# A two-phase MLP: up-projected tiles through DRAM, and a down-projection by seven block products for eight

## The chip, the cores and the metric

The kernel runs on one core of one Trainium2 chip. The metric is device microseconds of one execution. Before the change the median of three runs is 2024.57 us (2020.14 to 2024.82).

## What is computed

One layer of a decoder trunk, 1024 tokens of 1024 features, all in float32. Four token mixers run in parallel, are gated and projected back (`w_out`), and then comes an MLP. Only the MLP is changed:

```
h = rms_norm(x, g_mlp[l]) * (1.0 + sc2) + sh2
x = x + gt2 * (jnp.square(jax.nn.relu(h @ w_up[l])) @ w_down[l])
```

`w_up` is 1024 x 4096 (D_FF = 4096), `w_down` is 4096 x 1024. Both matrix products are made to float32 accuracy from three products of split operands: each operand is written as a high part (rounded to `fp32r`) and a low part (what is left), and high x high, high x low and low x high are summed.

## The kernel before

**The unit of TensorE work.** `split_product` (line 658) issues, for each 128-deep slice, three matmuls that stream 512 columns (lines 663, 664 and 665). Each matmul has a 128x128 weight load of its own. In the profile a matmul's name is "output<-one operand, other operand".

**Stages.** `stage_close` (line 676) is the last stage. It projects the mixers' results, multiplies by `w_out`, normalises and turns the token tiles (`turn`, `modulate`), and runs the MLP. Until the MLP begins nothing is changed but one DMA. The MLP has NB = 16 blocks of 256 hidden features, each of two feature tiles f of 128. Tokens are in two halves h of 512, the 1024 output columns in two halves c of 512, and TT = 8 token tiles of 128.

**Up-projection.** Blocks 0 and 1 ("plain") take all 8 block products of (feature tile) x (k half) x (token half). Blocks 2 to 15 take seven products P1, P6, P5, P7, P2, P3, P4 of 12 matmuls each (`up`, line 1222): sums of the quarter blocks of `w_up` (`sum_units`) times sums of the quarter blocks of h (`difference`, nine VectorE steps of 128x2048; `high_difference` on ScalarE and `low_difference` on VectorE split the four results into t_hi and t_lo). VectorE adds the seven results (`combine`), and the ReLU and the square follow.

**Down-projection.** `down` (line 1253) takes, for one block b, one column half c and one token tile, both feature tiles: 6 matmuls into one of four PSUM banks. `accumulate` (line 1513, the add is line 1521) adds the bank to the residual x1 in SBUF. That is 16 x 2 x 8 = 256 adds and 1536 matmuls. `w_down` is multiplied by the gate gt2 (`scale_unit`, line 1372) before it is split.

**What sets the order.** All queues are written out by hand. TensorE does plain(0), plain(1), and then for each b down(b) and up(b+2). A loaded weight block lies in a `tl_unit` buffer; ScalarE copies it to `tl_slot_hi` (`split_slot`, line 1021), and VectorE makes `tl_slot_lo` (`low_slot`, line 1377). There are six slots, used in a ring in the order of `ITEMS`. During down(b) VectorE slips the preparation of up(b+2) between the adds. All waits are on counting semaphores, and each engine does its list in order. SyncE (SP) issues all DMAs of the stage in order, so a DMA that waits holds back those behind it.

## Time and profile before

| | before |
|---|---|
| three runs, median | 2024.57 us (2020.14, 2024.57, 2024.82) |
| profiled execution: span from first to last instruction | 2020.5 us |
| TensorE busy | 1967.2 us (97%), 9416 matmuls recorded |
| VectorE busy | 1264.0 us (63%) |
| ScalarE busy | 706.4 us (35%) |
| DMA | 206.47 MB, mean 102 GB/s |
| TensorE clock, mean granted | 0.995 of full |

The page gives no time of the profiled execution other than its span. The span lies 0.4 us above the lowest of the three runs, 4.1 us below their median and 2.7 us below their mean of 2023.2.

How to read it: a matmul's shown duration (0.39 us) holds its passage through the array, which overlaps that of the next one. What a matmul costs a full queue is the distance between two starts. Counts of the program are taken from the code, since some matmul records can be missing. The MLP's down-projection begins 1400.8 us into the span.

### The profile page before, as it was taken

The page shows a single profiled execution, that of the slowest core. Times are in us where ns is not written, and L with a number is a line of the kernel's source. Part 1 is how long each engine was busy: PE and PEld are TensorE (multiplying, and loading weights), DVE is VectorE, ACT ScalarE, POOL GpSimd, SP SyncE. Part 2 cuts the span into 40 slices and gives each one's busy share as a digit, 9 for nine tenths or more (in the row PEclk, how much of TensorE's full clock was granted, in tenths as well). Part 3 has the DMA queues.
Part 4 walks back from the last instruction along what each step waited for, and adds up shares of the span by engine and source line. Part 5 has one row for each costly group of instructions (what it writes and reads, how often), then busy time and mean ns, then how long its engine had stood idle before and what let it go on. Part 6 is the DMA issues. An engine that isn't in the chain of part 4 may idle for free. (4 is left out here: it accounts for less than half of the span.)

```text
span 2020.5 us, 24310 instructions
## 1 busy us (share of the span) xinstructions
PE 1967.2 (97%) x9416; PEld 1584.5 (78%) x9416; DVE 1264.0 (63%) x1655; ACT 706.4 (35%) x1100; POOL 227.3 (11%) x136
## 2 busy tenths in 40 slices
PE   5999999999999999999999999999999999999999
PEld 4787888878766677877788788787888888888887
DVE  6546666101356476548457587669877777777776
ACT  5411212123466542166654443333232122222221
POOL 0121212112222144121101000000000000000000
PEclk9999999999999999999998999999999999999999
DMA  8354554224311252353122765301111111211112
GB/s 275 96 150 144 160 153 141 89 83 123 123 58 47 68 169 58 105 209 120 47 75 83 257 229 182 115 11 59 57 52 60 47 47 48 68 48 48 48 42 94
DMA packets 197339, 206.47 MB, mean 102 GB/s; under 512 B 9402, under 2 KB 154938, under 8 KB 197226
## 3 DMA queue, kind: packets, MB, share of 16 engines
q1 hardware_dynamic: 197056, 204.85, 32.1%
q8 instruction: 76, 1.25, 0.3%
q14 instruction: 37, 0.30, 0.0%
q10 hardware_dynamic: 170, 0.07, 0.0%
HBM read 157.57 MB, written 47.32 MB: 101 GB/s over the span
## 5 line engine op out<-in xcount | busy, mean ns | idle before, releaser
L663 PE MATMUL dn_ps<-h_hi,dn_hi 128*128 128x512 f32 (+1 forms) x1120 | 453.0, 404 | 15.2 <-PEq L60 4.8
L665 PE MATMUL dn_ps<-h_hi,dn_lo 128*128 128x512 f32 (+1 forms) x1120 | 439.7, 393 | 0.0
L664 PE MATMUL dn_ps<-h_lo,dn_hi 128*128 128x512 f32 (+1 forms) x1120 | 439.5, 392 | 0.0
L663 PEld LDWEIGHTS dn_ps<-h_hi,dn_hi 128*128 128x128 f32 (+1 forms) x1120 | 210.5, 188 | 83.2 <-issue 32.6
L665 PEld LDWEIGHTS dn_ps<-h_hi,dn_lo 128*128 128x128 f32 (+1 forms) x1120 | 210.4, 188 | 47.6
L139 POOL TENSOR_TENSOR dn_lo<-dn_raw,dn_hi 128x1024 fp32r<-128x1024 f32 (+1 forms) x69 | 172.4, 2499 | 661.6 <-ACT dn_hi L135 661.6
L664 PEld LDWEIGHTS dn_ps<-h_lo,dn_hi 128*128 128x128 f32 (+1 forms) x1120 | 210.7, 188 | 43.2 <-issue 1.2
L1521 DVE TENSOR_TENSOR tl_x<-tl_x,mg_ps_y 128x512 f32<-128x512 f32 x256 | 176.0, 688 | 89.4 <-PE mg_ps_y L665 82.7
L156 ACT ACTIVATE dn_out<-dn_ps 128x512 f32<-128x512 f32 (+1 forms) x138 | 81.8, 592 | 422.7 <-PE dn_ps L665 401.6
L663 PE MATMUL mg_ps_y<-tl_slot_hi,tl_u_hi 128*128 128x512 f32 x480 | 187.1, 390 | 1.2 <-issue 1.2
L665 PE MATMUL mg_ps_y<-tl_slot_hi,tl_u_lo 128*128 128x512 f32 x480 | 186.9, 389 | 0.0
L664 PE MATMUL mg_ps_y<-tl_slot_lo,tl_u_hi 128*128 128x512 f32 x480 | 186.8, 389 | 0.0
L1021 ACT ACTIVATE tl_slot_hi<-tl_unit 128x512 fp32r<-128x512 f32 x128 | 77.7, 624 | 134.4 <-DVE tl_unit L1372 108.8
L555 DVE SCALAR_TENSOR_TENSOR ada_sum<-ada,cols,ada_sum 128x256 f32<-128x256 f32 (+1 forms) x140 | 105.6, 754 | 4.7
L663 PEld LDWEIGHTS mg_ps_y<-tl_slot_hi,tl_u_hi 128*128 128x128 f32 x480 | 90.1, 188 | 20.7 <-issue 2.0
L665 PEld LDWEIGHTS mg_ps_y<-tl_slot_hi,tl_u_lo 128*128 128x128 f32 x480 | 90.1, 188 | 18.7
L664 PEld LDWEIGHTS mg_ps_y<-tl_slot_lo,tl_u_hi 128*128 128x128 f32 x480 | 90.1, 188 | 18.6
L1377 DVE TENSOR_TENSOR tl_slot_lo<-tl_unit,tl_slot_hi 128x512 fp32r<-128x512 f32 x128 | 86.5, 689 | 24.8 <-ACT tl_slot_hi L1021 24.8
L1021 ACT ACTIVATE tl_slot_hi<-tl_unit_sum 128x512 fp32r<-128x512 f32 x42 | 26.5, 632 | 172.9 <-DVE tl_unit_sum L1360 146.9
L1071 ACT ACTIVATE tl_u_hi<-tl_square 128x512 fp32r<-128x512 f32 x60 | 33.3, 621 | 142.5 <-PE mg_ps_y L665 127.2
L561 DVE TENSOR_TENSOR mod<-ps_m,cols 128x2 f32<-128x2 f32 x24 | 3.5, 158 | 117.7 <-PE ps_m L474 117.7
L135 ACT ACTIVATE dn_hi<-dn_raw 128x1024 fp32r<-128x1024 f32 (+1 forms) x71 | 73.7, 1040 | 6.1 <-DMA dn_raw<-w_in_dram 6.1
(390 smaller groups left out, 3468.6 us busy)
## 6 DMA issues: line engine op xcount, KB each, us to landing
dn_raw<-w_in_dram SPq DMA_DIRECT2D x70, 512.0 KB, 4.4
ada<-w_ada_dram SPq DMA_DIRECT2D x24, 1024.0 KB, 7.9
proj<-dn_out SPq DMA_DIRECT2D x72, 256.0 KB, 2.3
logits<-dn_out SPq DMA_DIRECT2D x64, 256.0 KB, 2.3
tl_unit<-w_up_dram SPq DMA_DIRECT2D x64, 256.0 KB, 2.9
tl_unit<-w_down_dram SPq DMA_DIRECT2D x64, 256.0 KB, 2.8
mg_gate<-logits SPq DMA_DIRECT2D x19, 512.0 KB, 4.7
wa_qk<-proj SPq DMA_DIRECT2D x6, 1024.0 KB, 8.3
```

The lines of the kernel that those rows point to most:

```text
L135: self.nc.scalar.activation(self.hi_at(j), self.raw_at(j), ACT.Copy).then_inc(self.hi_ready, 1)
L139: self.nc.gpsimd.tensor_tensor(self.lo_at(j), self.raw_at(j), self.hi_at(j).bitcast(F32), ALU.subtract).then_inc(self.lo_ready, 1)
L156: self.nc.scalar.activation(self.out[0:width, h, :], self.ps[0:width, h, :], ACT.Copy).then_inc(self.copied, 1)
L555: ins = nc.vector.scalar_tensor_tensor(out=total, in0=part, scalar=ck, in1=total, op0=ALU.mult, op1=ALU.add)
L561: last = nc.vector.tensor_tensor(k.mod[:, m:m + ADA_COLS], ps_m[:, m:m + ADA_COLS], k.cols[:, V_BADA + m:V_BADA + m + ADA_COLS], ALU.add)
L663: nc.tensor.matmul(out, w_hi[:, t, :], x_hi[:, t, :], start=begin, stop=False, skip_group_check=reopened)
L664: nc.tensor.matmul(out, w_hi[:, t, :], x_lo[:, t, :], start=False, stop=False, skip_group_check=reopened)
L665: mm = nc.tensor.matmul(out, w_lo[:, t, :], x_hi[:, t, :], start=False, stop=end, skip_group_check=reopened)
L1021: nc.scalar.activation(slot_hi[slot(j)][:, :, :], src, ACT.Copy).then_inc(slot_hi_ready, 1)
L1071: nc.scalar.activation(hidden_at(u_hi, b)[:, f, h * HALF:(h + 1) * HALF], square[:, f, h, :], ACT.Copy).then_inc(u_hi_ready, 1)
L1377: nc.vector.tensor_tensor(slot_lo[slot(j)][:, :, :], unit_at(kind, b, key), slot_hi[slot(j)][:, :, :].bitcast(F32), ALU.subtract).then_inc ...
L1521: nc.vector.tensor_tensor(x1[:, tt, cols], x1[:, tt, cols], bank(4 + n % 4), ALU.add).then_inc(summed, 1)
```

## The change

- **Phase one** makes all hidden blocks. The order on TensorE is plain(0), plain(1), then for b = 2, 3, ...: the first four products of b and the last three of b-1, into PSUM banks 0 to 3 for even b and 4 to 7 for odd b. ScalarE does ReLU and square (`finish`), VectorE makes four sums S1 to S4 of a block's four quarters (`sum_hidden`). Three quarters and the four sums, 7 x 256 KB a block, are stored to a DRAM scratch (`store_hidden`).
- **Phase two** is 7 products x 16 blocks = 112 steps of 12 matmuls (4 token tiles x 3). In step n product i = n // 16 adds block t = n % 16. The product stays in four PSUM banks for 16 steps, or for more where products are summed in place. A step needs a hidden tile, loaded from DRAM into one of three `raw_hidden` buffers, and a 128x512 piece of `w_down` or of its sums (`cell`; the sums are made in place by `turn_down`, 64 VectorE operations in steps 14 to 77). Both are split into a ring of nine pairs of buffers (`high_hidden`, `high_cell` on ScalarE; `low_hidden`, `low_cell` on VectorE). `w_down` stays in 64 cells in SBUF and is loaded once.
- **Eviction**: `keep` (ScalarE) and `evict_down` (VectorE) read the banks at the steps of `EVICT_AT`, multiply by the gate (which now is applied here and is saved in DRAM in between) and add to x1. The last four steps are done token tile by token tile. The last eviction is two dependent VectorE operations and then the store.

The diff, cut:

```diff
+        raw_hidden = [at(f"tl_raw_hidden{i}", kb, [P, HALF]) for i, kb in enumerate((64, 66, 68))]
+        kept = at("tl_kept", 0, [P, 4, HALF])
...
+        FIRST_PART, SECOND_PART = (P1, P6, P5, P7), (P2, P3, P4)
         ITEMS = [("plain", b, (f, kh)) for b in range(PLAIN) for f in range(BF) for kh in range(2)]
-        for b in range(NB):
-            ITEMS += [("down", b, (c, f)) for c in range(NH) for f in range(BF)]
-            if b + PLAIN < NB:
-                ITEMS += [("up", b + PLAIN, (p,)) for p in range(7)]
-        FIRST_DOWN = 4 * PLAIN
+        FIRST_UP = len(ITEMS)
+        for b in range(PLAIN, NB + 1):
+            ITEMS += [("up", b, (p,)) for p in FIRST_PART if b < NB]
+            ITEMS += [("up", b - 1, (p,)) for p in SECOND_PART if b > PLAIN]
         PLACE = {item: j for j, item in enumerate(ITEMS)}
+        A11, A12, A22, S1, S2, S3, S4 = range(7)
+        W11, W12, W21, W22 = range(4)
+        DOWN = [(A11, W11), (A12, W21), (S2, W11), (S3, W12), (S1, W11), (S4, W22), (A22, W21)]
+        BY_EVEN = (0, 2, 3, 6)
...
+        NEEDS = sorted([(t, W11, t) for t in range(NB)] + [(NB + t, W21, t) for t in range(NB)]
+                       + [(SUMS_FROM + 2 * t, w, t) for t in range(NB) for w in (W22, W12)])
+        LOAD_OF = {need[1:]: i for i, need in enumerate(NEEDS)}
...
+        EVICT_AT = {36: (1, 0), 39: (1, 1), 42: (1, 2), 45: (1, 3), 52: (2, 0), 54: (2, 1), 56: (2, 2), 58: (2, 3),
+                    68: (3, 0), 71: (3, 1), 74: (3, 2), 77: (3, 3), 84: (4, 0), 86: (4, 1), 88: (4, 2), 90: (4, 3),
+                    100: (5, 0), 102: (5, 1), 104: (5, 2), 106: (5, 3)}
...
+        def wait_ring(eng, m):
+            if m >= 9:
+                eng.wait_ge(step_done, (m - 9) // 2 + 1)
+            elif m in (4, 5):
+                eng.wait_ge(slot_lo_ready, PLACE["up", NB - 1, (P4,)] + 1)
+            else:
+                b, p = {0: (15, P6), 1: (14, P2), 2: (14, P3), 3: (14, P4), 6: (15, P2), 7: (15, P3), 8: (15, P4)}[m]
+                eng.wait_ge(up_done, up_count(b, p))
...
+            def store_hidden(b):
+                sp.wait_ge(quad_ready[0], b + 1)
+                sp.dma_start(k.hidden[A11, b], square[b % 2][:, 0, 0, :]).then_inc(quads_stored[b % 2], 16)
+                sp.wait_ge(quad_ready[1], b + 1)
+                sp.wait_ge(quad_ready[3], b + 1)
+                sp.dma_start(k.hidden[A12:A22 + 1, b].rearrange("s p t -> p s t"), square[b % 2][:, 1]).then_inc(quads_stored[b % 2], 16)
+                sp.wait_ge(hidden_summed, 4 * (b + 1))
+                sp.dma_start(k.hidden[S1:S4 + 1, b].rearrange("s p t -> p s t"), hidden_sum[:, :, :]).then_inc(sums_stored, 16)
+            def load_hidden(n):
+                i, t = n // NB, n % NB
+                a = DOWN[i][0]
+                if n < 3:
+                    sp.wait_ge(slot_lo_ready, PLACE["up", NB - 2, (P3,)] + 1)
+                else:
+                    sp.wait_ge(ring_lo_ready, 2 * (n - 3) + 1)
+                if a <= A22:
+                    sp.wait_ge(quads_stored[t % 2], 32 * (t // 2 + 1))
+                else:
+                    sp.wait_ge(sums_stored, 16 * (t + 1))
+                sp.dma_start(raw_hidden[n % 3][:, :], k.hidden[a, t]).then_inc(hidden_in[n % 3], 16)
...
+            for b in range(PLAIN, NB):
+                if b >= PLAIN + 1 and b + 1 < NB:
+                    load_ups(b + 1)
+                store_hidden(b - PLAIN)
+            for n in range(3):
+                load_hidden(n)
...
+            def finish(b, f, h):
+                q = 2 * f + h
+                own = square[b % 2][:, f, h, :]
...
                 else:
+                    if q == 0:
+                        act.wait_ge(up_done, up_count(b, P2))
+                        act.wait_ge(quads_stored[b % 2], 32 * (b // 2))
+                        act.wait_ge(hidden_summed, 4 * (b - 1))
+                        nc.scalar.activation(own, bank_of(b, 0), ACT.Relu).then_inc(clipped[0], 1)
+                    else:
+                        act.wait_ge(combined[{1: 3, 2: 4, 3: 2}[q]], nth(b))
+                        nc.scalar.activation(own, own, ACT.Relu).then_inc(clipped[q], 1)
+                    act.wait_ge(clipped[q], nth(b))
+                nc.scalar.activation(own, own, ACT.Square).then_inc(quad_ready[q], 1)
...
+            def high_hidden(n):
+                act.wait_ge(hidden_in[n % 3], 16 * (n // 3 + 1))
+                wait_ring(act, 2 * n)
+                nc.scalar.activation(ring_hi[2 * n % 9][:, :], raw_hidden[n % 3][:, :], ACT.Copy).then_inc(ring_hi_ready, 1)
+            def high_cell(n):
+                i, t = n // NB, n % NB
+                w = DOWN[i][1]
+                if i in (0, 1, 5):
+                    wait_cell(act, w, t)
+                else:
+                    act.wait_ge(turned_down, {2: 2 * t + 2, 3: 2 * t + 1, 4: 2 * NB + 2 * t + 2, 6: 2 * NB + 2 * t + 1}[i])
+                wait_ring(act, 2 * n + 1)
+                nc.scalar.activation(ring_hi[(2 * n + 1) % 9][:, :], cell(w, t)[:, :], ACT.Copy).then_inc(ring_hi_ready, 1)
...
+            for p in FIRST_PART[2:4]:
+                split_slot("up", PLAIN, (p,))
             high_difference(3)
+            for b in range(PLAIN, NB + 1):
+                if b > PLAIN:
+                    split_slot("up", b - 1, (P2,))
+                if b > PLAIN + 1:
+                    finish(b - 2, 1, 0)
+                    finish(b - 2, 0, 1)
+                if b > PLAIN:
+                    split_slot("up", b - 1, (P3,))
+                    split_slot("up", b - 1, (P4,))
+                if b < NB:
+                    take_first(b)
+                if b > PLAIN:
+                    finish(b - 1, 1, 1)
                 if b + 1 < NB:
+                    for p in FIRST_PART:
                         split_slot("up", b + 1, (p,))
+                if PLAIN < b < NB:
+                    finish(b - 1, 0, 0)
+            for n in range(3):
+                high_hidden(n)
+                high_cell(n)
+            finish(NB - 1, 0, 0)
+            high_hidden(3)
+            high_cell(3)
+            finish(NB - 1, 1, 0)
+            finish(NB - 1, 0, 1)
+            for n in range(4, STEPS):
+                high_hidden(n)
+                if n - 3 in (NB, 3 * NB, 5 * NB):
+                    keep((n - 3) // NB - 1)
+                high_cell(n)
...
+            def down(n, tt):
+                i, t = n // NB, n % NB
                 cols = slice(tt * P, (tt + 1) * P)
-                for f in range(BF):
-                    j = PLACE["down", b, (c, f)]
-                    pe.wait_ge(slot_lo_ready, j + 1)
-                    last = split_product(nc, bank(4 + n % 4), hidden_at(u_hi, b)[:, f:f + 1, cols], hidden_at(u_lo, b)[:, f:f + 1, cols],
-                                         flat(slot_hi[slot(j)]).unsqueeze(1), flat(slot_lo[slot(j)]).unsqueeze(1), first=(f == 0), last=(f == BF - 1))
-                last.then_inc(down_done, 1)
+                if t == 0:
+                    wait_down_bank(i, tt)
+                pe.wait_ge(ring_lo_ready, 2 * n + 2)
+                a, w = 2 * n % 9, (2 * n + 1) % 9
+                return split_product(nc, down_bank(i, tt), ring_hi[a][:, cols].unsqueeze(1), ring_lo[a][:, cols].unsqueeze(1),
+                                     ring_hi[w][:, :].unsqueeze(1), ring_lo[w][:, :].unsqueeze(1), first=(t == 0 and i not in (2, 3, 5)),
+                                     last=(t == NB - 1), reopened=i in (2, 3, 5))
...
+            for kind, b, key in ITEMS[FIRST_UP:]:
+                up(b, key[0])
+            for n in range(STEPS - LAST_STEPS):
+                for tt in range(4):
+                    last = down(n, tt)
+                    if n % NB == NB - 1 and tt < 3:
+                        last.then_inc(bank_done, 1)
+                last.then_inc(step_done, 1)
+            for tt in range(4):
+                for n in range(STEPS - LAST_STEPS, STEPS):
+                    last = down(n, tt)
+                last.then_inc(bank_done if tt < 3 else step_done, 1)
...
+            def sum_hidden(b):
+                a11, a21, a12, a22 = (square[b % 2][:, f, h, :] for f in range(BF) for h in range(NH))
+                s1, s2, s3, s4 = (hidden_sum[:, n, :] for n in range(4))
                 for q in range(4):
+                    dve.wait_ge(quad_ready[q], b + 1)
                 if b >= 1:
+                    dve.wait_ge(sums_stored, 16 * b)
                 else:
+                    dve.wait_ge(up_done, 4 * PLAIN)
+                nc.vector.tensor_tensor(s1, a21, a22, ALU.add).then_inc(hidden_summed, 1)
+                nc.vector.tensor_tensor(s3, a11, a21, ALU.add).then_inc(hidden_summed, 1)
+                dve.wait_ge(hidden_summed, 4 * b + 1)
+                nc.vector.tensor_tensor(s2, a11, s1, ALU.add).then_inc(hidden_summed, 1)
+                dve.wait_ge(hidden_summed, 4 * b + 3)
+                nc.vector.tensor_tensor(s4, a12, s2, ALU.add).then_inc(hidden_summed, 1)
...
             difference(8)
+            low_difference(1)
+            for n in (1, 2, 3):
+                sum_units(PLAIN, n)
+            for p in (P1, P6):
+                low_slot("up", PLAIN, (p,))
+            low_difference(2)
+            sum_units(PLAIN, 4)
+            for p in (P5, P7):
+                low_slot("up", PLAIN, (p,))
             difference(9)
+            low_difference(3)
+            for b in range(PLAIN, NB + 1):
+                if b > PLAIN:
+                    low_slot("up", b - 1, (P2,))
+                if b > PLAIN + 1:
+                    combine(b - 2, 5)
+                    combine(b - 2, 4)
+                if b > PLAIN:
+                    low_slot("up", b - 1, (P3,))
+                    low_slot("up", b - 1, (P4,))
+                if b < NB:
+                    combine(b, 1)
+                sum_hidden(b - 2)
+                if b + 1 < NB:
+                    for n in (1, 2, 3):
+                        sum_units(b + 1, n)
+                    for p in (P1, P6):
+                        low_slot("up", b + 1, (p,))
+                    sum_units(b + 1, 4)
+                    for p in (P5, P7):
+                        low_slot("up", b + 1, (p,))
+                if b < NB:
+                    combine(b, 2)
+                    combine(b, 3)
+            for n in range(3):
+                low_hidden(n)
+                low_cell(n)
+            combine(NB - 1, 5)
+            combine(NB - 1, 4)
+            low_hidden(3)
+            low_cell(3)
+            sum_hidden(NB - 1)
+            for n in range(4, STEPS):
+                where = EVICT_AT.get(n)
+                if where:
+                    evict_down(*where, 0)
+                if 0 <= n - SUMS_FROM < 4 * NB:
+                    turn_down(n - SUMS_FROM)
+                if where:
+                    evict_down(*where, 1)
+                low_hidden(n)
+                if where:
+                    evict_down(*where, 2)
+                low_cell(n)
+                if where:
+                    evict_down(*where, 3)
+            for tt in range(4):
+                evict_down(6, tt, 0)
+                evict_down(6, tt, 1)
```

Two places of the order show it. On **TensorE**, after the last matmuls of plain(1), before the change (names: `tl_u` is the hidden block, `tl_slot` a weight block):

```order
L665 MATMUL mg_ps_y<-tl_h_hi,tl_slot_lo_9659 128x512
L663 MATMUL mg_ps_y<-tl_slot_hi_9650,tl_u_hi 128x512
L664 MATMUL mg_ps_y<-tl_slot_lo_9656,tl_u_hi 128x512
L665 MATMUL mg_ps_y<-tl_slot_hi_9650,tl_u_lo 128x512
```

and with the change:

```order
L665 MATMUL mg_ps_y<-tl_h_hi,tl_slot_lo_9659 128x512
L663 MATMUL dn_ps<-tl_h_hi,tl_slot_hi_9650 128x512
L664 MATMUL dn_ps<-tl_h_lo,tl_slot_hi_9650 128x512
L665 MATMUL dn_ps<-tl_h_hi,tl_slot_lo_9656 128x512
```

The 96 matmuls of down(0) that stood between plain(1) and the first product of block 2 are gone from this place.

On **VectorE**, before the change, from the last `difference` on (L1445 is `low_difference`, L1357 to L1363 `sum_units`):

```order
L1441 TENSOR_TENSOR tl_t_full_9683<-tl_t_full_9683,tl_h_lo 128x2048
L1445 TENSOR_TENSOR tl_t_lo_9677<-tl_t_full_9681,tl_t_hi_9673 128x2048
L1445 TENSOR_TENSOR tl_t_lo_9678<-tl_t_full_9682,tl_t_hi_9674 128x2048
L1521 TENSOR_TENSOR tl_x_9643<-tl_x_9643,mg_ps_y 128x512
L1445 TENSOR_TENSOR tl_t_lo_9679<-tl_t_full_9683,tl_t_hi_9675 128x2048
L1521 TENSOR_TENSOR tl_x_9643<-tl_x_9643,mg_ps_y 128x512 x2
```

and with the change, from `low_slot` of P5 and P7 of block 2 to `low_slot` of P1 of block 3 (L1558 is `low_slot`, L1622 and L1626 the last `difference` and `low_difference`, L1635 `combine`, L1662 to L1667 `sum_hidden`, L1542 to L1548 `sum_units`):

```order
L1558 TENSOR_TENSOR tl_slot_lo_9658<-tl_unit_sum_9672,tl_slot_hi_9652 128x512
L1558 TENSOR_TENSOR tl_slot_lo_9659<-tl_unit_9664,tl_slot_hi_9653 128x512
L1622 TENSOR_TENSOR tl_t_full_9685<-tl_t_full_9685,tl_h_lo 128x2048
L1626 TENSOR_TENSOR tl_t_lo_9681<-tl_t_full_9685,tl_t_hi_9677 128x2048
L1635 TENSOR_TENSOR tl_first_product_9689<-tl_first_product_9689,dn_ps 128x512
L1662 TENSOR_TENSOR tl_hidden_sum<-tl_square_9686 128x512
L1663 TENSOR_TENSOR tl_hidden_sum<-tl_square_9686 128x512
L1665 TENSOR_TENSOR tl_hidden_sum<-tl_square_9686,tl_hidden_sum 128x512
L1667 TENSOR_TENSOR tl_hidden_sum<-tl_square_9686,tl_hidden_sum 128x512
L1542 TENSOR_TENSOR tl_unit_sum_9672<-tl_unit_9670,tl_unit_9671 128x512
L1545 TENSOR_TENSOR tl_unit_sum_9673<-tl_unit_sum_9672,tl_unit_9668 128x512
L1548 TENSOR_TENSOR tl_unit_9670<-tl_unit_9668,tl_unit_9670 128x512
L1558 TENSOR_TENSOR tl_slot_lo_9660<-tl_unit_9668,tl_slot_hi_9654 128x512
```

Two long and eight short operations now stand between the slots of block 2 and the first slot of block 3.

On **ScalarE**, with the change, the last three `split_slot` of phase one (L1152), with `finish` (L1196 the ReLU, L1198 the square) of block 14 between them; for blocks 2 to 15 the three products that they serve are P2, P3 and P4:

```order
L1152 ACTIVATE tl_slot_hi_9655<-tl_unit_9669 128x512
L1196 ACTIVATE tl_square_9686<-tl_square_9686 128x512
L1198 ACTIVATE tl_square_9686<-tl_square_9686 128x512
L1196 ACTIVATE tl_square_9686<-tl_square_9686 128x512
L1198 ACTIVATE tl_square_9686<-tl_square_9686 128x512
L1152 ACTIVATE tl_slot_hi_9650<-tl_unit_9668 128x512
L1152 ACTIVATE tl_slot_hi_9651<-tl_unit_9671 128x512
```

Before the change VectorE did the squares, and a down-projection stood between the up-projections of two blocks; now the last three products of block 14 and of block 15 follow one another with nothing between.

## Rows read from the trace of the kernel before

**Rows 1.** The page, engines in total and the groups of instructions (line, engine, names, count | busy, mean ns | idle before).

```profile
PE 1967.2 (97%) x9416; PEld 1584.5 (78%) x9416; DVE 1264.0 (63%) x1655; ACT 706.4 (35%) x1100; POOL 227.3 (11%) x136
...
L1521 DVE TENSOR_TENSOR tl_x<-tl_x,mg_ps_y 128x512 f32<-128x512 f32 x256 | 176.0, 688 | 89.4 <-PE mg_ps_y L665 82.7
```

**Rows 2.** Stretch 1500 to 1600 us, busy time by engine, clock, DMA share, GB/s.

```profile
1500.00:1600.00 100.00, 100.00 (x443) 82.81 (x442) 76.45 (x119) 25.06 (x44) 0.00 (x0) 1.00 0.18 56
```

**Rows 3.** All waits of TensorE from 1300 us to the end.

```profile
PE mg_ps_y L1208 <- DVE tl_xn L1397: 2.1, 2, 1.5
PE mg_ps_y L663 <- issue: 1.2, 1, 1.2
```

**Rows 4.** Timeline of TensorE, first and last of 28 matmuls in a row (start, us).

```profile
1499.72 0.39 PE L663 MATMUL mg_ps_y<-tl_slot_hi,tl_u_hi 128*128 128x512 f32 x1
...
1505.84 0.39 PE L663 MATMUL dn_ps<-tl_h_hi,tl_slot_hi 128*128 128x512 f32 x1
```

**Rows 5.** The tile tl_u_hi: TensorE's matmuls on it, first and last start.

```profile
L663 PE MATMUL mg_ps_y<-tl_slot_hi,tl_u_hi x480: 388/389/468, 1400.8 to 1994.8; 128*128 128x512 f32 x160
```

**Rows 6.** Timeline of VectorE around the start of down(0) and in up(2).

```profile
1398.84 2.29 DVE L1441 TENSOR_TENSOR tl_t_full<-tl_t_full,tl_h_lo 128x2048 f32<-128x2048 f32 x1
1401.05 4.49 DVE L1445 TENSOR_TENSOR tl_t_lo<-tl_t_full,tl_t_hi 128x2048 fp32r<-128x2048 f32 x2
...
1426.44 2.50 DVE L1484 TENSOR_TENSOR tl_u_lo<-tl_square,tl_u_hi 128x512 fp32r<-128x512 f32 x4
...
1435.37 0.68 DVE L1458 TENSOR_TENSOR tl_square<-tl_first_product,mg_ps_y 128x512 f32<-128x512 f32 x1
1436.08 0.69 DVE L1461 TENSOR_TENSOR tl_square<-tl_square,mg_ps_y 128x512 f32<-128x512 f32 x1
```

**Rows 7.** Timeline of ScalarE in the same stretch.

```profile
1398.30 0.60 ACT L1057 ACTIVATE tl_square<-mg_ps_y 128x512 f32<-128x512 f32 x1 [2.50 <-PE mg_ps_y L665]
1401.16 1.92 ACT L1075 ACTIVATE tl_t_hi<-tl_t_full 128x2048 fp32r<-128x2048 f32 x1 [2.27 <-DVE tl_t_full L1441]
...
1425.77 2.20 ACT L1071 ACTIVATE tl_u_hi<-tl_square 128x512 fp32r<-128x512 f32 x4 [8.91 <-DVE tl_square L1478]
```

**Rows 8.** TensorE after idle times elsewhere: timeline, and stretches with the clock.

```profile
39.34 0.80 PE L663 MATMUL dn_ps<-h_hi,dn_hi 128*128 128x512 f32 x1 [4.33 <-DVE h_lo L578]
39.94 0.63 PE L664 MATMUL dn_ps<-h_lo,dn_hi 128*128 128x512 f32 x1
...
44.63 0.47 PE L663 MATMUL fr_open_ps<-h_hi,dn_hi_x 128*128 128x512 f32 x1
...
902.53 0.47 PE L663 MATMUL dn_ps<-h_hi,dn_hi 128*128 128x512 f32 x1 [2.50 <-PEq L60]
902.84 0.39 PE L664 MATMUL dn_ps<-h_lo,dn_hi 128*128 128x512 f32 x1
...
1085.67 0.72 PE L1907 MATMUL wa_ps_second<-ident,wa_prob 128*128 128x128 f32 x3 [2.06 <-ACT wa_probT L1852]
...
1086.00:1088.00 2.00, 2.00 (x12) 2.00 (x10) 2.00 (x1) 0.51 (x1) 1.46 (x1) 0.50 0.70 205
...
1094.00:1096.00 2.00, 2.00 (x6) 1.61 (x6) 1.83 (x12) 0.00 (x0) 0.00 (x0) 0.50 0.00 0
```

**Rows 9.** DMA issues (count, KB, us to landing), and a stretch with many in flight.

```profile
tl_unit<-w_down_dram SPq DMA_DIRECT2D x64, 256.0 KB, 2.8
...
mix<-cv_acc SPq DMA_DIRECT2D x1, 1024.0 KB, 7.8
...
mix<-sb_yT SPq DMA_DIRECT2D x1, 1024.0 KB, 4.3
...
0.00:25.00 25.00, 9.95 (x41) 8.02 (x41) 11.37 (x23) 15.10 (x32) 1.26 (x10) 1.00 0.99 325
```

**Rows 10.** The end: last matmul and last add, from the timelines of both engines.

```profile
2016.97 0.39 PE L665 MATMUL mg_ps_y<-tl_slot_hi,tl_u_lo_last 128*128 128x512 f32 x1
...
2017.40 0.69 DVE L1521 TENSOR_TENSOR tl_x<-tl_x,mg_ps_y 128x512 f32<-128x512 f32 x1 [0.67 <-PE mg_ps_y L665]
```

541 lines of the change are left out of this document (287 added, 254 removed).

## The prediction, made before the changed kernel ran

> **What bounds the kernel now.** I read the engine totals first, then a stretch of the MLP, then TensorE's waits, then the distance of its matmuls. TensorE is busy 97% of the span, VectorE 63%, and VectorE's idle time before the adds of the down-projection is spent waiting for TensorE [rows 1]. Between 1500 and 1600 us TensorE is busy 100.00 of 100.00 us at full clock while VectorE has 24 us free, ScalarE 75, and the DMA engines are used to 18% [rows 2]. From 1300 us to the end TensorE waits 3.3 us in all [rows 3]. So the MLP takes the number of matmuls times their distance. That distance is 6.12 us over 27 matmuls, 0.2268 us, the same in down- and up-projections, which follow each other in that stretch [rows 4]. The MLP's part from down(0) on begins at 1400.8 [rows 5] and the last matmul starts at 2016.97 [rows 10]: 616.2 us for 2711 steps of 0.2268 = 614.9, and 1.3 us more, which is the wait for "issue" [rows 3]. Matmuls are the only currency here, as long as everything else stays hidden.
>
> **What is removed.** The down-projection has 16 x 2 x 8 x 6 = 1536 matmuls before, and 112 x 12 = 1344 after. The up-projection keeps its count. 192 matmuls x 0.2268 = **43.5 us** less. VectorE's 256 adds [rows 1], its 64 gate multiplications and the splitting of hidden blocks in phase one go too. They were hidden and are worth nothing by themselves.
>
> **Prices of the added work.** A VectorE operation on 128x512 occupies the engine 0.60 us when the next is independent (four take 2.50, the last 0.69), and 0.71 when the next reads its result; one on 128x2048 2.29 [rows 6]. A ScalarE operation on 128x512 takes 0.52 to the next and about 0.62 to its result (four take 2.20), one on 128x2048 1.92 [rows 7]. A signal from TensorE reaches another engine about 0.2 us after the next matmul could have started. This follows from the last matmul at 2016.97 and its add at 2017.40, 0.43 later [rows 10]. A product or step is 12 matmuls, T = 2.72 us.
>
> **Phase one in its steady part.** Per block of 7 products (19.05 us) VectorE has 7 low slots, 4 sums of weights, 5 combinations and 4 hidden sums, 20 operations or 12 to 14 us. ScalarE has 16, or 8.5 to 10. The orders leave each weight slot ready three products or more before its use. DMA moves 4 loads and 7 stored quarters of 256 KB, 2.9 MB per 19.05 us, 151 GB/s, where 325 has been moved [rows 9]. Cost: nothing. Cover: the lead of three products.
>
> **The start of phase one: a stall.** Before, the 96 matmuls of down(0), 21.8 us, hid the end of the `difference` chain. Now block 2 begins at 1400.8 and P1 of block 3, four products later, wants to start at 1411.7. VectorE, in order: P5's slot of block 2 can be written only when TensorE leaves the slot, at 1400.8. ScalarE sees that at 1401.0, does ReLU and square of block 1 (0.65 and 0.52), then the split, done at 1402.8. Two low slots (1.2) put `difference(9)` at 1404.1. It takes 2.29, ScalarE's high part 1.92 and hand-overs 0.08, so `low_difference(3)` starts at 1408.4. Then come 2.2 for it, one combination (0.6), four hidden sums (0.6, 0.6, 0.7, 0.6), three sums of weights (0.7, 0.6, 0.6), and the low slot of P1 (0.69). This slot is ready at 1416.3. **Stall 4.7 us** (bounds: 0 if some operations overlap better, 7 if the DMAs of the new weights are late too). Later slots of block 3 follow at 0.6 to 1.2 and need 2.72.
>
> **The clock after it.** After 4.33 us of idleness in the front stage the following 11 matmul distances were 0.43 us, from 39.94 to 44.63, and then 0.23 again; after 2.50 us of idleness following dense work the distance was 0.23 at once; after 2.06 us following small matmuls the granted clock was 0.50 until 1096 [rows 8]. So 12 matmuls at 0.43 cost 12 x 0.20 = **2.4 us**, the value that I take since the idle time is nearest. The ends are 0 (the row at 902.53) and 5 (half of the ten us at 0.50). The Trainium skill ("TensorE: Matmul & The Clock Gate", Part 1) holds that the half-rate clock is the default and sustained activity lifts it. By that rule a cold start after this stall is to be expected, and it gives no reason for the fast restart at 902.53.
>
> **The end of phase one: a second stall.** The last products of block 14 and block 15 are neighbours. The slot of P3(15) comes, on ScalarE, behind `finish` of two quarters of block 14, whose sums can be made only when P4(14) is done. From there: 0.2 signal, 0.7 combination, 0.63 ReLU, 0.54 square, 0.63 ReLU, 0.54 square, 0.63 split, 0.73 low slot: 4.7 us, where TensorE needs it after one product, 2.72. **Stall 2.0 us**, too short for the clock if the 2.50 row holds. In all other blocks four products of the next block lie between, so the same chain is hidden.
>
> **The first steps of phase two.** Steps 0 to 3 are prepared under P3 and P4 of block 15. Step 4 is behind `sum_hidden(15)`, which waits for ScalarE's last squares and for the 1 MB store of S1 to S4 of block 14. Such a store took 4.3 or 7.8 us [rows 9]. My count has step 4 ready 0 to 1 us late. I take **0.5**, bounds 0 and 4.
>
> **Steady phase two.** VectorE has two low parts a step and in steps 14 to 77 one sum, 3 x 0.60 = 1.8 of 2.72 us; with the densest eviction (4 operations in 3 steps, steps 68 to 79) 2.6 plus dependent pairs, about even with TensorE, and nearly three steps of ring stand against it. ScalarE has 1.1. A hidden tile's cycle with three buffers is landing + split + low part, 2.8 [rows 9] + 1.5 = 4.3 us in three steps, 8.2. Changes of product wait for `keep`, which runs bank by bank under the other banks. Cost: nothing.
>
> **The tail.** The last eviction is two dependent operations instead of one: **0.7 us**.
>
> **The small parts**: saving the gate adds one 512 KB store during the branch merging, where DMA has room; nothing.
>
> **Sum.** -43.5 + 4.7 + 2.4 + 2.0 + 0.5 + 0.7 = -33.2 us. Against the profiled span, 2020.5 - 33.2 = 1987.3. The median of the runs shown is 4.1 above that span, their mean 2.7; I add 2.7 and predict **1990.0 us**.
>
> **Rivals.**
> - *No stalls*: the orders overlap better than I count and the whole 43.5 us stay. 2020.5 - 43.5 = 1977, or 1980 for the runs. Against it: the list of VectorE operations between the slots is fixed. Chance 0.12.
> - *A bound in the middle of phase two*: in steps 14 to 31 a step loads a hidden tile and two cells, 786 KB in 2.72 us, 289 GB/s. 325 were moved for 25 us by transfers of up to 1 MB [rows 9]. If 256 KB transfers reach only 240, those 16 steps take 3.3 us each, 9 us more, and the evictions at steps 68 to 79 may add 3. Result 2002, up to 2008 with longer stalls at the change of phase. Chance 0.17.
> - *Slower*: the transfers of one step run one after another, not side by side. Three at 2.8 us [rows 9] are 8.4 us a step; the 16 steps then cost 16 x 5.7 = 91 us more, 2081. It decides from 33/16 = 2.1 us more a step, that is when DMA gives less than 164 GB/s there. Against it: 325 GB/s in the first 25 us, on the same queue. The Trainium skill ("DMA: Bandwidth & Descriptors", Bandwidth) advises transfers of 1 MiB and more for three quarters of the peak, which speaks against this change's 256 KB pieces; its fit of about 2.0 us plus bytes / 436 GB/s gives an estimate of 2.6 us for one of them alone, and if nothing overlapped the sum would be near this rival's. Chance 0.06.
> - *The matmuls saved are no time*: the new waits take back all of it (within 0.3%, 6 us, about what a measurement of this kernel can tell). It would need some 30 us of stalls beyond those counted, 0.27 us at every step of phase two. Chance 0.05.
>
> The forecast itself has 0.60. **Range**: 1978 to 2008. It holds the forecast with its bounds (1982 to 2000), most of the no-stall case and the middle rival; left out are the last two rivals and the edges. Faster 0.89, the same 0.05, slower 0.06.
>
> **What the profile after would show.** 192 matmuls fewer, distance 0.227 in both phases; down-projection about 304.8 us in 112 steps. TensorE's waits: one on `tl_slot_lo` of about 4.7 us near 1412, with half clock for 2 to 5 us behind it, one of 2 us some 250 us later on `tl_slot_lo`, and little on `tl_ring_lo`. The last add would end about 1.8 us after the start of the last matmul (0.43 + 0.71 + 0.69). It would be wrong if TensorE waits on `tl_ring_lo` in every step (DMA landings above 6.7 us in steps 14 to 31, or VectorE at its limit from 14 to 77), if the distance of the matmuls rises though nothing waits, or if the wait near 1412 is absent.

## The result and the profile after

The changed kernel took **1988.78 us** (median of four runs, 1987.47 to 1990.35) beside 2022.36 us for the kernel before (2020.00 to 2024.82): ratio 0.9829, 95% interval 0.9815 to 0.9843. Its profiled execution has a span of 1988.6 us. The prediction was 1990.0 us, and 1987.3 for the span.

The page of the changed kernel, engines in total (busy us, share, instructions), two groups of the MLP (busy, mean ns | idle before), and the DMA issues of the MLP (count, KB each, us to landing):

```profile
PE 1927.7 (97%) x9224; PEld 1551.3 (78%) x9224; DVE 1191.7 (60%) x1555; ACT 831.3 (42%) x1314; POOL 227.2 (11%) x136
...
L1227 ACT ACTIVATE tl_ring_hi<-tl_cell 128x512 fp32r<-128x512 f32 x112 | 70.6, 630 | 140.7 <-PE mg_ps_y L665 126.5
...
L1217 ACT ACTIVATE tl_ring_hi<-tl_raw_hidden 128x512 fp32r<-128x512 f32 x112 | 69.3, 619 | 21.2 <-DMA tl_raw_hidden<-hidden 21.1
...
tl_raw_hidden<-hidden SPq DMA_DIRECT2D x112, 256.0 KB, 2.7
...
tl_unit<-w_up_dram SPq DMA_DIRECT2D x64, 256.0 KB, 3.2
hidden<-tl_hidden_sum SPq DMA_DIRECT2D x16, 1024.0 KB, 4.9
tl_cell<-w_down_dram SPq DMA_DIRECT2D x64, 256.0 KB, 5.1
```

TensorE has 192 matmuls fewer than in [rows 1] and is still busy 97% of the span. VectorE lost 72 us of work, ScalarE gained 125; neither shows in the time. Read the two groups by what released them. ScalarE's splits for phase two were idle 126.5 us waiting for TensorE to leave a slot of the ring, and only 21.1 us for a hidden block to land. So TensorE sets the pace of phase two and the transfers don't.

All waits of TensorE from 1300 us to the end (us in all, count, longest), the counterpart of [rows 3]:

```profile
PE mg_ps_y L663 <- DVE tl_slot_lo L1558: 6.3, 2, 4.5
PE mg_ps_y L1377 <- DVE tl_xn L1578: 2.1, 2, 1.5
PE dn_ps L663 <- DVE tl_ring_lo L1699: 0.5, 1, 0.5
```

The waits on `tl_xn` were there before. The 1.2 us for "issue" are not there any more. New are two waits on `tl_slot_lo`, 4.5 and 1.8 us, and 0.5 us on the ring. The timeline of TensorE shows where (start, length, wait in brackets):

```profile
1364.25 1.09 PE L1377 MATMUL mg_ps_y<-ident,tl_xn 128*128 128x128 f32 x8 [0.58 <-DVE tl_xn L1578]
...
1418.80 0.80 PE L663 MATMUL mg_ps_y<-tl_h_hi,tl_slot_hi 128*128 128x512 f32 x1 [4.46 <-DVE tl_slot_lo L1558]
1419.39 0.63 PE L664 MATMUL mg_ps_y<-tl_h_lo,tl_slot_hi 128*128 128x512 f32 x1
...
1423.97 0.39 PE L663 MATMUL mg_ps_y<-tl_t_hi,tl_slot_hi 128*128 128x512 f32 x1
...
1673.51 0.50 PE L663 MATMUL mg_ps_y<-tl_h_hi,tl_slot_hi 128*128 128x512 f32 x1 [1.82 <-DVE tl_slot_lo L1558]
...
1690.66 0.50 PE L663 MATMUL dn_ps<-tl_ring_hi,tl_ring_hi 128*128 128x512 f32 x1 [0.54 <-DVE tl_ring_lo L1699]
...
1984.33 0.39 PE L665 MATMUL mg_ps_y<-tl_ring_hi,tl_ring_lo 128*128 128x512 f32 x1
```

The first stall is in front of P1 of block 3, the second in front of P3 of block 15. The 12 matmuls of P1(3) take 5.17 us, from 1418.80 to 1423.97, instead of 12 x 0.2268 = 2.72: that is the price of the clock, 2.45 us. The windows of the same kernel show it (us; busy and count of PE, PEld, DVE, ACT, POOL; granted clock, DMA share, GB/s), and below them phase two where it loads most:

```profile
1416.00:1418.00 2.00, 0.00 (x0) 0.00 (x0) 1.97 (x4) 0.35 (x1) 0.00 (x0) 0.75 0.44 163
1418.00:1420.00 2.00, 1.20 (x3) 1.01 (x4) 2.00 (x5) 2.00 (x5) 0.00 (x0) 0.50 1.00 290
1420.00:1422.00 2.00, 2.00 (x7) 1.52 (x6) 1.97 (x4) 0.36 (x1) 0.00 (x0) 0.50 0.65 203
1422.00:1424.00 2.00, 2.00 (x7) 1.58 (x6) 1.67 (x3) 0.00 (x0) 0.00 (x0) 0.55 0.00 0
1424.00:1426.00 2.00, 2.00 (x10) 1.65 (x9) 0.69 (x1) 1.80 (x4) 0.00 (x0) 1.00 0.84 252
...
1700.00:1750.00 50.00, 50.00 (x223) 41.40 (x222) 35.30 (x56) 25.65 (x45) 0.00 (x0) 1.00 0.92 309
1750.00:1800.00 50.00, 50.00 (x222) 41.44 (x221) 42.09 (x68) 20.91 (x37) 0.00 (x0) 1.00 0.57 180
```

The stretch 1700 to 1750 moves 309 GB/s and TensorE is busy all of its 50.00 us at full clock. TensorE does steps 8 to 25 in it, and the loads run ahead: SyncE issues 37 cells and 20 hidden blocks there, as dense as the 36 and 18 that steps 14 to 31 need in 49 us. Phase two as a whole runs from the start of step 0's first matmul at 1679.1 to that of the last at 1984.33, 305.2 us for 1344 matmuls: 304.6 for 1343 distances, and the 0.5 us wait.

VectorE's timeline shows the chain behind the first stall:

```profile
1406.52 2.28 DVE L1622 TENSOR_TENSOR tl_t_full<-tl_t_full,tl_h_lo 128x2048 f32<-128x2048 f32 x1
...
1410.79 2.29 DVE L1626 TENSOR_TENSOR tl_t_lo<-tl_t_full,tl_t_hi 128x2048 fp32r<-128x2048 f32 x1 [1.98 <-ACT tl_t_hi L1212]
1413.00 0.68 DVE L1635 TENSOR_TENSOR tl_first_product<-tl_first_product,dn_ps 128x512 f32<-128x512 f32 x1
...
1418.06 0.68 DVE L1558 TENSOR_TENSOR tl_slot_lo<-tl_unit,tl_slot_hi 128x512 fp32r<-128x512 f32 x1
...
1985.48 0.69 DVE L1755 TENSOR_TENSOR tl_x<-tl_x,tl_gated_product 128x512 f32<-128x512 f32 x1
```

VectorE is not short of time. It is busy with a list in a poor order: `low_difference(3)`, a combination and four hidden sums stand ahead of the slot that TensorE wants at 1414.3. The slot is finished at 1418.74, and P1(3) starts at 1418.80. The last row ends at 1986.17, 1.84 us after the last matmul's start; before it was 1.12 [rows 10].

**A sum from trace to trace.** The front stages, which nobody changed, differ by some us between executions, so I measure from the first TensorE instruction of the last token tile's turn to the end. Before that is 2020.5 - 1361.77 = 658.7 us, after it 1988.6 - 1364.25 = 624.35: **34.4 us less**. The parts: -43.5 matmuls, +4.5 and +2.45 for the first stall and its clock, +1.8, +0.5, +0.7 for the tail, -1.2 for the "issue" wait gone, together -34.75. The front of this execution is 2.5 us later, which is why the whole span shows only 31.9.

### The profile page after: what moved, and what is told of

It is laid out like the page before. It is cut to its first block and busy times, and to the rows that moved or that the text cites. A ratio compares the mean times of both kernels' runs of the same rounds, so it can differ in the third digit from the quotient of the medians.

```text
span 1988.6 us, 24178 instructions
## 1 busy us (share of the span) xinstructions
PE 1927.7 (97%) x9224; PEld 1551.3 (78%) x9224; DVE 1191.7 (60%) x1555; ACT 831.3 (42%) x1314; POOL 227.2 (11%) x136
## 5 line engine op out<-in xcount | busy, mean ns | idle before, releaser
L1227 ACT ACTIVATE tl_ring_hi<-tl_cell 128x512 fp32r<-128x512 f32 x112 | 70.6, 630 | 140.7 <-PE mg_ps_y L665 126.5
L664 PE MATMUL mg_ps_y<-tl_ring_lo,tl_ring_hi 128*128 128x512 f32 x320 | 124.6, 389 | 0.0
L663 PE MATMUL mg_ps_y<-tl_ring_hi,tl_ring_hi 128*128 128x512 f32 x320 | 124.6, 389 | 0.0
L665 PE MATMUL mg_ps_y<-tl_ring_hi,tl_ring_lo 128*128 128x512 f32 x320 | 124.6, 389 | 0.0
L1699 DVE TENSOR_TENSOR tl_ring_lo<-tl_cell,tl_ring_hi 128x512 fp32r<-128x512 f32 x112 | 77.3, 690 | 64.6 <-ACT tl_ring_hi L1227 63.8
L1558 DVE TENSOR_TENSOR tl_slot_lo<-tl_unit,tl_slot_hi 128x512 fp32r<-128x512 f32 x78 | 52.2, 689 | 60.5 <-ACT tl_slot_hi L1152 60.5
L1694 DVE TENSOR_TENSOR tl_ring_lo<-tl_raw_hidden,tl_ring_hi 128x512 fp32r<-128x512 f32 x112 | 76.8, 686 | 12.6 <-ACT tl_ring_hi L1217 12.3
L1217 ACT ACTIVATE tl_ring_hi<-tl_raw_hidden 128x512 fp32r<-128x512 f32 x112 | 69.3, 619 | 21.2 <-DMA tl_raw_hidden<-hidden 21.1
L665 PE MATMUL mg_ps_y<-tl_t_hi,tl_slot_lo 128*128 128x512 f32 x196 | 76.3, 389 | 0.0
L664 PE MATMUL mg_ps_y<-tl_t_lo,tl_slot_hi 128*128 128x512 f32 x196 | 76.3, 389 | 0.0
L663 PE MATMUL mg_ps_y<-tl_t_hi,tl_slot_hi 128*128 128x512 f32 x196 | 76.3, 389 | 0.0
```

The lines of the kernel that those rows point to most:

```text
L663: nc.tensor.matmul(out, w_hi[:, t, :], x_hi[:, t, :], start=begin, stop=False, skip_group_check=reopened)
L664: nc.tensor.matmul(out, w_hi[:, t, :], x_lo[:, t, :], start=False, stop=False, skip_group_check=reopened)
L665: mm = nc.tensor.matmul(out, w_lo[:, t, :], x_hi[:, t, :], start=False, stop=end, skip_group_check=reopened)
L1217: nc.scalar.activation(ring_hi[2 * n % 9][:, :], raw_hidden[n % 3][:, :], ACT.Copy).then_inc(ring_hi_ready, 1)
L1227: nc.scalar.activation(ring_hi[(2 * n + 1) % 9][:, :], cell(w, t)[:, :], ACT.Copy).then_inc(ring_hi_ready, 1)
L1558: nc.vector.tensor_tensor(slot_lo[slot(j)][:, :, :], unit_at(kind, b, key), slot_hi[slot(j)][:, :, :].bitcast(F32), ALU.subtract).then_inc ...
```

## The experiments

The theory: TensorE's matmuls are the only currency, and the stalls at the two changes of phase come from the order of work on VectorE and ScalarE. Rivals: the saving has another source, VectorE as a whole is too slow there, or the transfers of phase two are near their limit. "The sum" below is the stretch just defined, from one profiled execution of each kernel; the changed kernel has 624.35. In a second execution of the same kernel (experiment 5) it is 624.9, so differences of about 0.5 us say nothing.

**1. VectorE's order at the start of phase one.** `low_difference(3)`, `combine(2, 1)` and `sum_hidden(0)` go behind the four low slots of block 3.

```diff
             difference(9)
-            low_difference(3)
...
-                if b < NB:
+                if PLAIN < b < NB:
                     combine(b, 1)
-                sum_hidden(b - 2)
+                if b > PLAIN:
+                    sum_hidden(b - 2)
...
+                if b == PLAIN:
+                    low_difference(3)
+                    combine(b, 1)
+                    sum_hidden(b - 2)
```

(`sum_units` waits in block 3 for one low slot in addition, since the order no longer implies it.)

> At the start of phase one VectorE prepares block 3 (sums of weights and four low slots) before low_difference(3), combine and sum_hidden(0). Theory (time is matmuls x 0.2268 us plus three stalls): the wait of 4.5 us before P1(3) and the 12 slow matmuls behind it (2.6 us) both go, about 7 us less than the changed kernel, some 1981.6 us; no wait on tl_slot_lo but the one of 1.8 us near the end of phase one. Rival (the start is bound by the DMA of the new weights or by the ReLU of block 1, VectorE only shows it): the wait stays, with another releaser, and the time stays within 1 us of 1988.8. A third case: P4(2) now waits for t_lo of the fourth difference, 1 to 3 us back.

Measured 1980.15 us (1977.02 to 1984.69), ratio 0.9791 (0.9774 to 0.9808), an interval that lies apart from the changed kernel's. TensorE's waits in the MLP's part:

```profile
PE mg_ps_y L663 <- DVE tl_slot_lo L1560: 1.8, 1, 1.8
...
PE dn_ps L663 <- DVE tl_ring_lo L1701: 0.5, 1, 0.5
```

The 4.5 us wait is gone, and with it the slow clock: the sum is 617.4, 7.0 us less, for 4.5 + 2.45. No operation was saved, only the order changed, so the stall was one of order and not of VectorE's speed.

**2. ScalarE's order at the end of phase one.** The splits for P3(15) and P4(15) go ahead of `finish` of block 14.

```diff
-                if b > PLAIN + 1:
+                if PLAIN + 1 < b < NB:
                     finish(b - 2, 1, 0)
                     finish(b - 2, 0, 1)
                 if b > PLAIN:
                     split_slot("up", b - 1, (P3,))
                     split_slot("up", b - 1, (P4,))
+                if b == NB:
+                    finish(b - 2, 1, 0)
+                    finish(b - 2, 0, 1)
```

> In the last round of phase one ScalarE splits P3(15) and P4(15) before the ReLUs and squares of block 14. Theory: the wait of 1.8 us before P3(15) goes; the step 4 wait of 0.5 us stays or grows by up to 1, so 1 to 2 us less than the changed kernel, about 1987. Rival (the slot is late because of VectorE's combinations): the wait shrinks by less than half, no change.

Measured 1988.27 us, ratio 0.9830 (0.9815 to 0.9845): no difference from the changed kernel. Its waits of TensorE say why:

```profile
PE mg_ps_y L663 <- DVE tl_slot_lo L1561: 4.5, 1, 4.5
...
PE dn_ps L663 <- DVE tl_ring_lo L1702: 2.1, 1, 2.1
```

The wait before P3(15) is gone, but that at step 4 grew from 0.5 to 2.1 us. `finish` of block 14 only moved behind the splits, and TensorE reaches step 4 earlier. The two small stalls share one chain, ScalarE's and VectorE's finishing of two blocks, so the one takes back what the other gives: 1.8 us of waiting gone, 1.6 come back. The sum fell by 0.85, hardly more than two executions of one kernel differ.

**3. Work in the place of a wait.** One more product, 12 matmuls, is issued before P1(3) into the bank that P1(3) then starts anew; its result is dropped.

```diff
                 j = PLACE["up", b, (p,)]
+                if b == PLAIN + 1 and p == P1:
+                    pe.wait_ge(relu_ready, 4 * (b - 1))
+                    for _ in range(1):
+                        split_product(nc, bank_of(b, 0), t_hi[0][:, :, 0:P], t_lo[0][:, :, 0:P], t_hi[2], t_lo[2])
                 pe.wait_ge(slot_lo_ready, j + 1)
```

> TensorE does one more product of 12 matmuls (results overwritten by P1(3)) in the 4.5 us in which it would wait for P1(3)'s slot: the wait falls to about 1.7 us, the product starts when it did before. Theory (the clock falls in the long wait and costs 12 slow matmuls): the granted clock stays at 1.0, the 12 matmuls take 2.7 instead of 5.1 us, 2.4 us less than the changed kernel though work was added, about 1986.4. Rival (the slow matmuls come from something else, such as the load of weights or the DMA burst at that moment): they stay slow, and the time is the same 1988.8.

Measured 1983.84 us (1983.04 to 1987.52), ratio 0.9811 (0.9797 to 0.9826), the sum 622.1: with 12 matmuls more, the kernel is 2.3 us quicker by the sum. (By the medians it is 4.9, but the two intervals of the ratio overlap.) TensorE's timeline and the window at that place:

```profile
1418.28 0.50 PE L663 MATMUL mg_ps_y<-tl_h_hi,tl_slot_hi 128*128 128x512 f32 x1 [1.74 <-DVE tl_slot_lo L1562]
1418.61 0.39 PE L664 MATMUL mg_ps_y<-tl_h_lo,tl_slot_hi 128*128 128x512 f32 x1
...
1418.00:1420.00 2.00, 1.72 (x8) 1.42 (x8) 2.00 (x5) 1.85 (x4) 0.00 (x0) 1.00 0.98 279
```

The slot comes as late as before, but the idle time is cut to 1.74 us and the clock stays at 1.00. This isolates the clock's share of the stall, 2.3 us against 2.45 read from the timeline. The Trainium skill ("TensorE: Matmul & The Clock Gate", Part 1) says that the half-rate clock is the default and sustained activity lifts it. The trace agrees as far as it goes: the clock is 0.50 behind the wait of 4.46 us and 1.00 behind that of 1.74.

**4. As many matmuls as before.** In 64 steps of phase two the first token tile's three matmuls are issued twice, 192 more in all. The output then holds these products twice on that token tile.

```diff
                     last = down(n, tt)
+                    if tt == 0 and n in [m for m in range(STEPS) if 0 < m % NB < NB - 1][:64]:
+                        last = down(n, tt)
```

> Phase two gets back 192 matmuls: in 64 of the steps the first token tile's 3 matmuls are done twice (the output is not the reference's there). Theory (matmuls are the only currency): 43.5 us more than the changed kernel, 2032.3 us, that is above the kernel before by its stalls, about 10 us. Rival (the gain comes from the 256 adds, the gate multiplications or the better order of the rest): the time stays clearly under 2022, and TensorE waits less elsewhere.

Measured 2027.77 us (2027.09 to 2032.81), ratio 1.0029 (1.0016 to 1.0041); the sum is 667.1, 42.8 us above the changed kernel. That is 43.5 for 192 matmuls less the 0.5 us at step 4, which vanished; the 6.3 us on `tl_slot_lo` are unchanged. By the medians it is 39.0 us, and the expected 2032.3 is missed by 4.5; the mark lies 5.7 us earlier in this profiled execution than in the changed kernel's, and only the sum is free of that. So by the sum the whole gain is the number of matmuls, and everything else in the change costs: with equal matmuls the sum is 8.4 us above the kernel before.

**5. The changed kernel once more**, beside experiments 6, 7 and 8.

> The changed kernel once more, beside the next one on the same chip. Every theory expects 1988.8 us, ratio 0.983 to before, and the same three waits of TensorE behind the last turn of a token tile: 4.5, 1.8 and 0.5 us.

Measured 1986.34 us (1985.44 to 1990.49), ratio 0.9825 (0.9811 to 0.9838), the sum 624.9, the same two waits of 6.3 us together and 0.7 us at step 4.

**6. All the orders at once.** Experiments 1 and 2, and the `finish` and `sum_hidden` of block 15 two steps later:

```diff
-            finish(NB - 1, 1, 0)
-            finish(NB - 1, 0, 1)
             for n in range(4, STEPS):
+                if n == 6:
+                    finish(NB - 1, 1, 0)
+                    finish(NB - 1, 0, 1)
...
-            sum_hidden(NB - 1)
             for n in range(4, STEPS):
+                if n == 6:
+                    sum_hidden(NB - 1)
```

> The orders of e1 and e2 together, and the ReLU, square and sums of block 15 put behind the preparation of steps 4 and 5. Theory (three separate stalls and a slow clock behind the first): all of 4.5 + 2.6 + 1.8 + 0.5 = 9.4 us go, about 1979.4 us, ratio 0.978; TensorE waits for nothing from the last turn to the end. Rival (the stalls hide one another, as in the run that reordered the end, where the wait of 1.8 came back as 1.6 us at step 4): 1.5 to 2 us of waiting on tl_ring_lo remain in steps 4 to 6.

Measured **1978.76 us** (1974.75 to 1981.63), ratio 0.9783 (0.9769 to 0.9798), an interval that lies apart from that of run 5. The sum is 614.4. The only wait of TensorE from 1340 us on, and the stretches where the stalls had been:

```profile
PE mg_ps_y L1381 <- DVE tl_xn L1584: 0.6, 1, 0.6
...
1400.00:1450.00 50.00, 50.00 (x222) 41.24 (x221) 40.80 (x60) 23.60 (x40) 0.00 (x0) 1.00 0.47 147
...
1650.00:1700.00 50.00, 50.00 (x222) 41.42 (x221) 31.73 (x51) 27.75 (x50) 0.00 (x0) 1.00 0.92 316
```

Nothing is left between the matmuls in the whole MLP's part. This version is faster than both kernels and leaves nothing out. It is 9.9 us below the changed kernel by the sum, for 4.5 + 2.45 + 1.8 + 0.5 = 9.25. Against experiment 1 alone it gains 2.9 by the sum, but the two intervals of the ratio overlap.

**7. Two buffers for the hidden blocks instead of three**, so that a hidden block's landing, split and low part must fit into two steps, 5.4 us.

```diff
-        raw_hidden = [at(f"tl_raw_hidden{i}", kb, [P, HALF]) for i, kb in enumerate((64, 66, 68))]
+        raw_hidden = [at(f"tl_raw_hidden{i}", kb, [P, HALF]) for i, kb in enumerate((64, 66))]
...
-                    sp.wait_ge(ring_lo_ready, 2 * (n - 3) + 1)
+                    sp.wait_ge(ring_lo_ready, 2 * (n - 2) + 1)
```

> raw_hidden has two buffers instead of three, so a hidden tile's cycle (landing + split + low part) has 2 steps, 5.4 us, instead of 8.2. Theory (cycle 2.7 + 1.5 = 4.2 us with an idle queue, landings of 3.5 to 5 us while the cells are loaded in steps 12 to 31): little in most steps, and 0 to 1 us a step in steps 12 to 31, so 0 to 15 us more than 1988.8, and TensorE's waits on tl_ring_lo lie before 1765 us. Rival (the ring of nine pairs, not the landings, sets the pace of preparation): no change at all.

Measured 1994.10 us (two runs, 1993.91 and 1994.28), ratio 0.9859 (0.9841 to 0.9877), the sum 627.5, 3.2 above the changed kernel. TensorE's waits on the ring, the place of the longer one, the clock behind it, and the landing of the hidden blocks between 1700 and 1750 us:

```profile
PE dn_ps L663 <- DVE tl_ring_lo L1699: 2.4, 2, 1.9
...
1692.52 0.50 PE L663 MATMUL dn_ps<-tl_ring_hi,tl_ring_hi 128*128 128x512 f32 x1 [1.93 <-DVE tl_ring_lo L1699]
...
1694.00:1696.00 2.00, 2.00 (x6) 1.60 (x5) 0.77 (x2) 1.41 (x3) 0.00 (x0) 0.50 0.40 141
...
tl_raw_hidden<-hidden SPq DMA_DIRECT2D x18, 256.0 KB, 3.9
```

Both waits are in the first five steps of phase two, where the third buffer had given a start. In steps 12 to 31, the dense ones, TensorE never waits. A tile's cycle there is 3.9 us to land and 1.5 for split and low part, 5.4 together, which is just what two steps hold. So here the third buffer was worth its start and no more.

**8. Two matmuls for three in phase two.** The product of the low part of the hidden with the high part of the weights is left out, 448 matmuls fewer; the output is less exact. It asks how far phase two is from its next bound.

```diff
-                return split_product(nc, down_bank(i, tt), ring_hi[a][:, cols].unsqueeze(1), ring_lo[a][:, cols].unsqueeze(1),
...
+                nc.tensor.matmul(down_bank(i, tt), ring_hi[a][:, cols], ring_hi[w][:, :], start=(t == 0 and i not in (2, 3, 5)), stop=False,
...
+                return nc.tensor.matmul(down_bank(i, tt), ring_hi[a][:, cols], ring_lo[w][:, :], start=False, stop=(t == NB - 1),
```

> Phase two leaves out the low x high matmul of every product (448 fewer, the output loses accuracy). If TensorE were still the bound a step would take 1.81 us and the time would fall by 101.6 us to 1887. Theory: VectorE (1.8 us a step from step 14 to 77, 2.6 with evictions) and the DMA (786 KB a step from 14 to 31, 2.4 us at 325 GB/s) take over, so it falls by 75 to 95 us only, 1894 to 1914, with TensorE waiting on tl_ring_lo in steps 14 to 80. Rival (the cover of phase two is thin, a little less matmul work already exposes it everywhere): it falls by less than 50 us.

Measured 1925.06 us (1923.23 to 1926.88), ratio 0.9518 (0.9500 to 0.9535), the sum 59.6 below the changed kernel. That misses the expectation of 75 to 95. 448 x 0.2268 = 101.6 us of matmuls went, and 42 came back. TensorE's waits of phase two and three stretches of it:

```profile
PE dn_ps L1444 <- DVE tl_ring_lo L1700: 13.5, 10, 3.3
PE mg_ps_y L1444 <- DVE tl_ring_lo L1700: 11.5, 10, 2.5
...
PE dn_ps L1444 <- ACT tl_kept L1239: 2.7, 1, 2.7
...
1700.00:1720.00 20.00, 17.52 (x73) 12.78 (x72) 15.90 (x26) 12.36 (x23) 0.00 (x0) 1.00 1.01 365
...
1760.00:1780.00 20.00, 14.98 (x63) 11.56 (x64) 19.86 (x33) 10.26 (x18) 0.00 (x0) 1.00 0.56 170
...
1820.00:1840.00 20.00, 16.03 (x61) 11.98 (x60) 19.69 (x33) 9.22 (x16) 0.00 (x0) 0.91 0.35 105
```

27.7 us are waits. In the second stretch VectorE is busy 19.86 of 20.00 us while the DMA engines are used to 56%; it is busy 19.5 us or more in every 20 from 1740 to 1840, and there the next bound is VectorE. Some 9 us of the waits come before that, up to 1735. There it looks like the transfers: in the first stretch the DMA engines are full, at 365 GB/s, and VectorE is busy 15.90 us. No experiment separates the two. The last stretch shows a clock of 0.91 besides. Of the other 14 us about 7 are the slow clock: 36 matmuls start more than 0.40 us after the one before with no wait listed, and have 7.3 us over their 0.2268 each. The rest is small delays, at the restarts and between.

**9. One transfer at a time in phase two.** SyncE waits for the landing of each load before it issues the next, which makes the slower rival's condition true.

```diff
                 sp.dma_start(raw_hidden[n % 3][:, :], k.hidden[a, t]).then_inc(hidden_in[n % 3], 16)
+                sp.wait_ge(hidden_in[n % 3], 16 * (n // 3 + 1))
...
+                sp.wait_ge(down_in[i % 8], 16 * (i // 8 + 1))
```

> SyncE waits for each load of phase two to land before it issues the next, so transfers never overlap. Theory of the forecast (loads overlap, and that is what keeps phase two hidden): 49 cells and 108 hidden tiles one after another at 2.3 to 2.8 us each are 360 to 440 us where phase two has 305, so 60 to 140 us more than 1988.8; the kernel is then slower than before (over 2040 us), most of it in steps 12 to 45. Rival (landings are mostly waiting in the queue behind others, one alone lands in under 1.5 us): less than 20 us more.

Measured 2161.34 us (2159.78 to 2162.91), ratio 1.0701 (1.0658 to 1.0744), the sum 175.3 above the changed kernel: more than expected. TensorE's waits of phase two, ten loads of cells on SyncE's queue (start, length of the ten), the first long wait of TensorE, and a stretch:

```profile
PE dn_ps L663 <- DVE tl_ring_lo L1701: 68.0, 12, 31.5
PE mg_ps_y L663 <- DVE tl_ring_lo L1701: 56.2, 12, 7.4
...
PE dn_ps L663 <- ACT tl_kept L1241: 4.5, 1, 4.5
...
1680.12 23.58 SPq L1025 DMA_DIRECT2D tl_cell<-w_down_dram  x10
...
1716.34 0.79 PE L663 MATMUL dn_ps<-tl_ring_hi,tl_ring_hi 128*128 128x512 f32 x1 [31.53 <-DVE tl_ring_lo L1701]
...
1750.00:1800.00 50.00, 26.97 (x78) 19.86 (x79) 11.55 (x19) 6.90 (x12) 0.00 (x0) 0.70 0.34 100
```

128.7 us are waits. 31.5 of them are one wait near the start of phase two, before step 3: ten cells, 2.36 us each, stand on SyncE's queue in front of the stores of block 14 and the next hidden blocks. No expectation had that. The stretch of the slower rival, from the first matmul of step 14 at 1765.7 to that of step 32 at 1900.6, takes 134.9 us where 18 steps at full pace take 49.0. That is 86 more, 61 of them waits. And TensorE, busy 26.97 of 50 us, has a granted clock of 0.70 there, so that the matmuls between two waits cost more as well: in all of phase two 181 matmuls start more than 0.40 us after the one before with no wait listed, and have 39 us over their 0.2268 each. Waits and slow clock together are 168 of the 175; small delays are the rest. The stretch moves 100 GB/s; the same loads side by side move 309 in the changed kernel. The rival's mechanism is real, and several transfers in flight are what keeps it away.

## Why the prediction was right

**What is removed, -43.5 us.** Right: phase two takes 305.2 us, the wait of 0.5 us included, where 304.8 was expected, and experiment 4 puts the 192 matmuls back at 42.8 us.

**The start of phase one, 4.7 us.** Measured 4.5. The list held step by step. Shifted by the 2.5 us by which this execution's front was later, the last `difference` was expected at 1406.6 and stood at 1406.52, `low_difference(3)` at 1410.9 and stood at 1410.79, the slot at 1418.8 and was ready at 1418.74. Experiment 1 removes it by order alone. (The prediction's own times, 1416.3 and 1411.7, lie 4.6 us apart and not 4.7.)

**The clock after it, 2.4 us.** Measured 2.45 in the timeline, 2.3 by experiment 3. The value taken was that of the idle time nearest in length, and that choice was right here. As a general guide it is weaker than it looks; see the last section.

**The end of phase one, 2.0 us, and step 4, 0.5 us.** Measured 1.8 and 0.5. (The items of the chain add up to 4.6 us and not 4.7, which gives 1.9.) What the prediction did not say is that the two hang on one chain: experiment 2 shows that the wait before P3(15), removed alone, comes back at step 4 but for 0.2 us.

**The tail, 0.7 us.** 1.84 - 1.12 = 0.72.

**The steady parts, nothing.** Right. In the whole phase two of the changed kernel TensorE waits once, 0.5 us. But one number of it was too low where it mattered: a hidden block took 2.7 us to land in the median of all, but 4.3 between 1700 and 1750 us, and a cell 5.0, as the DMA view of that stretch shows:

```profile
tl_cell<-w_down_dram SPq DMA_DIRECT2D x37, 256.0 KB, 5.0
...
tl_raw_hidden<-hidden SPq DMA_DIRECT2D x20, 256.0 KB, 4.3
```

The cycle of a hidden buffer is 4.3 + 1.5 = 5.8 us and not 4.3, still under the 8.2 of three steps. The 2.8 came from the single loads of a stage with little traffic.

**The sum.** -33.2 predicted, -34.4 measured from the last token tile's turn on. The difference of 1.2 is as large as the wait for "issue" of [rows 3], which I left in and which did not come back; the stalls were 0.35 us shorter than predicted, and as much stays unaccounted for. The front was 2.5 us later by chance and moved the span the other way, to 1988.6 where 1987.3 was expected. That the median of 1988.78 lies within 1.3 us of the predicted 1990.0 is in part luck too, since the front alone varies by more. The terms are borne out by the sum and the single waits, not by the median.

**The rivals.** *No stalls* fell: the stalls are in the trace, and experiment 6 shows what it would have been, by other orders. *A bound in the middle of phase two* fell by the stretch at 309 GB/s with TensorE busy all the time; its 240 GB/s was too low. (Steps 14 to 31 are 18 steps and not the 16 of its sum and of the next rival's, which makes 10 us of the 9 and 103 of the 91.) The Trainium skill ("DMA: Bandwidth & Descriptors", Bandwidth) advises 1 MiB and more a transfer for three quarters of the peak. The 256 KB pieces here did without: with several in flight they moved 309 to 316 GB/s over 50 us, all that the kernel asked for. The Trainium skill's fit ("DMA: Bandwidth & Descriptors", Anatomy of one DMA — SWDGE (gpsimd) path), from which the prediction took an estimate of 2.6 us for one such transfer, is stated for transfers issued by GpSimd; the ten issued by SyncE one after another in experiment 9 took 2.36 us each. *Slower* fell in the changed kernel and came true in experiment 9, at 175 us. Its own stretch, steps 14 to 31, cost 86 us against the 91 stated; the rest came through the queue at the start, the steps after 31 and the clock. *The matmuls saved are no time* fell by experiment 4.

## What to carry to other kernels

Where one engine is busy all the time, count its instructions and price them by their distance. Then look only at the seams, where one phase's tail and the next phase's head meet on an engine whose order is fixed: write down that engine's list between the last release and the operand that is missed, with 0.60 us for an independent operation on 128x512 and 0.71 for a dependent one, as in [rows 6]. A seam is mended by order, and stalls that hang on one chain together; where it can't be, work without use in the wait can keep the clock up, as in experiment 3. Before you cut further, ask which engine is next: in experiment 8, 42 of 102 us came back, with VectorE full from 1740 to 1840 us.

## What the runs showed that I had not expected

**A wait of 2 us may or may not cost the clock.** After 1.93 us in experiment 7 it fell to 0.50, with six matmuls in the 2.00 us of the window shown there. After 1.82 us (before P3(15)) and 2.1 us (experiment 2, at step 4) it stayed at full, as after 2.50 in [rows 8]. Here is the window behind that last one, TensorE idle for a third of it and at clock 1.00:

```profile
1690.00:1692.00 2.00, 1.27 (x6) 1.05 (x7) 2.00 (x5) 0.00 (x0) 0.00 (x0) 1.00 0.43 78
```

The length of the idle time alone does not decide. What does stays open; no run here was made to tell.

**The front varies.** The last token tile's turn begins between 1356.8 and 1365.5 us in executions of kernels that are the same up to there but for one store. That is more than most of the terms above. Without a mark inside the trace from which to measure, the 2.3 us of experiment 3 could not have been read. Even with it two executions of the changed kernel differ by 0.5 us, so the 0.85 of experiment 2 is at the limit of what it can tell.
